# Diagonal tap weights built by ScalarE instead of GpSimd, with three smaller reorderings, in a four-block decoder trunk

## The reference, cut to what matters

```python
for i in range(DEPTH):                       # DEPTH = 2
    x = layer_norm(ALPHA * x + 0.5 * swiglu(x, ffn1_w_gu[i], ffn1_w_down[i]), ...)
    if i % 2 == 0:
        y, qm = gla_mix(x @ gla_w_in, ...)   # gated linear attention
    else:
        y, qm = conv_mix(x @ conv_w_in, ...) # depthwise convolution of width 31, layer norm, silu
    m = mem_attention(qm, mem, mem_w_kv[i])
    x = layer_norm(ALPHA * x + concatenate([y, m]) @ w_out, ...)
    x = layer_norm(ALPHA * x + 0.5 * swiglu(x, ffn2_w_gu[i], ffn2_w_down[i]), ...)

def swiglu(x, w_gu, w_down):                 # w_gu is 1024 x 5632, w_down is 2816 x 1024
    a, b = split(x @ w_gu, 2)
    return (silu(a) * b) @ w_down
```

## Time and profile before

| | us |
|---|---|
| median of 3 runs | 2049.1 |
| lowest and highest | 2047.54 and 2049.7 |
| the profiled execution, its own time | 2050.35 |
| the span in its trace, first to last instruction | 2048.6 |
| TensorE busy in it | 2023.3 (99%) |
| VectorE busy | 1355.9 (66%) |
| ScalarE busy | 811.7 (40%) |
| GpSimd busy | 786.7 (38%) |

### The profile page before, as it was taken

One profiled execution on the slowest core, in us unless ns is written; L12 is line 12 of the kernel. 1 busy time (PEld: TensorE's weight loads), 2 busy tenths in 40 slices (PEclk: granted clock), 3 DMA queues, 4 the chain that ended last, 5 costly groups with the idle time before them and its releaser, 6 DMA issues.

```text
span 2048.6 us, 34293 instructions
## 1 busy us (share of the span) xinstructions
PE 2023.3 (99%) x13509; PEld 1856.2 (91%) x13509; DVE 1355.9 (66%) x1842; ACT 811.7 (40%) x1163; POOL 786.7 (38%) x443
## 2 busy tenths in 40 slices
PE   9999999999999999999999999999999999999998
PEld 9899998988988989999898999989887798999887
DVE  4477774554435768877456877646899886767645
ACT  5433452253423344444234444423353534434422
POOL 1499820033312257881015888001100225877000
PEclk9999999999999999999999999999999999999999
DMA  7545323332211234543232445323544322332232
GB/s 250 185 144 163 123 87 101 101 105 83 63 32 62 93 114 144 164 151 104 99 109 93 161 146 164 105 95 99 185 124 175 103 82 84 102 102 92 89 102 87
DMA packets 229497, 239.13 MB, mean 117 GB/s; under 512 B 5983, under 2 KB 222173, under 8 KB 227612
## 3 DMA queue, kind: packets, MB, share of 16 engines
q1 hardware_dynamic: 228764, 235.68, 35.3%
q10 hardware_dynamic: 640, 2.16, 0.3%
HBM read 215.80 MB, written 22.02 MB: 116 GB/s over the span
## 4 chain that ended last, share of the span: by engine, by line
PE 83%; DVE 5%; POOL 5%; issue 3%; ACT 2%; DMA 1%; DVEq 0%; SPq 0%; ACTq 0%; POOLq 0%
PE bank L1764 11%; PE bank L1766 11%; PE bank L1765 11%; PE bank L1893 10%; PE bank L1894 10%; PE bank L1895 10%; PE bank L1775 4%; PE bank L1776 3%; PE bank L1777 3%; DVE u L1680 2%; POOL xlo L531 1%; ACT whi L662 1%; POOL s L553 1%; POOL diag_tmp L585 1%; PE bank L1799 1%
## 5 line engine op out<-in xcount | busy, mean ns | idle before, releaser
L662 ACT CAST whi<-raw 128x2048 fp32r<-128x2048 f32 (+2 forms) x192 | 325.9, 1699 | 881.6 <-POOL scratch L560 436.4
L1113 DVE TENSOR_TENSOR wlo<-raw,whi 128x2048 fp32r<-128x2048 f32 (+2 forms) x166 | 358.4, 2159 | 243.9 <-ACT whi L662 243.6
L537 POOL TENSOR_TENSOR tiny<-tiny 128x2 f32<-128x2 f32 (+1 forms) x13 | 9.4, 724 | 754.3 <-DVE tiny L1389 754.3
L556 POOL TENSOR_TENSOR raw<-raw 128x512 f32<-128x512 f32 x72 | 220.4, 3062 | 0.0
L1764 PE MATMUL bank<-h_hi,whi 128*128 128x512 f32 x528 | 207.1, 392 | 0.0
L1765 PE MATMUL bank<-h_lo,whi 128*128 128x512 f32 x528 | 205.5, 389 | 0.0
L1766 PE MATMUL bank<-h_hi,wlo 128*128 128x512 f32 x528 | 205.5, 389 | 0.0
L1893 PE MATMUL bank<-t_hi,whi 128*128 128x256 f32 x576 | 163.9, 285 | 2.9 <-DVE bank L1181 2.9
L560 POOL TENSOR_TENSOR scratch<-raw,s 128x512 f32<-128x512 f32 x72 | 149.2, 2072 | 44.2 <-DVE ex_lo L1120 44.2
L1893 PE MATMUL bank<-t_hi,ex_hi 128*128 128x256 f32 x576 | 163.7, 284 | 0.7 <-DVE bank L1173 0.4
L1894 PE MATMUL bank<-xlo,whi 128*128 128x256 f32 x576 | 163.0, 283 | 0.0
(11 more groups left out here) (351 smaller groups left out, 5880.8 us busy)
## 6 DMA issues: line engine op xcount, KB each, us to landing
raw<-in_ffn_w_gu_dram SPq DMA_DIRECT2D x88, 1024.0 KB, 4.9
raw<-in_ffn_w_down_dram SPq DMA_DIRECT2D x32, 896.0 KB, 5.0
raw<-in_ffn_w_down_dram SPq DMA_DIRECT2D x32, 512.0 KB, 3.3
raw<-in_gla_w_in_dram SPq DMA_DIRECT2D x14, 1024.0 KB, 5.1
early_raw<-in_conv_w_in_dram SPq DMA_DIRECT2D x18, 512.0 KB, 4.2
lo_scratch<-early_lo SPq DMA_DIRECT2D x18, 512.0 KB, 3.2
diag_scratch<-diag_tmp SPq DMA_DIRECT2D x8, 1024.0 KB, 8.8
raw<-in_conv_w_in_dram SPq DMA_DIRECT2D x16, 512.0 KB, 5.4
```

The source lines that it names most:

```text
L556: nc.gpsimd.tensor_tensor(a21, a21, a11, ALU.add).then_inc(w_sum, 1)
L662: nc.scalar.copy(whi[:, s, 0:kc, 0:width], raw[:, s, 0:kc, 0:width]).then_inc(hi_ready, 1)
L1113: nc.vector.tensor_tensor(wlo[:, s, 0:kc, 0:width], raw[:, s, 0:kc, 0:width], whi[:, s, 0:kc, 0:width].bitcast(F32), ALU.subtract).then_in ...
```

## The change

There are four parts.

1. **Second tile of mem_w_kv by halves.** It is loaded, rounded, subtracted and used in two halves, as the first one already is.
2. **x_sums.** All four sums of a block wait until x is complete in hi and lo part. Before, in blocks 1 to 3, sum 0 waited for the hi parts of the first half of x alone and sum 1 for all hi parts and half of the lo parts. Sums 2 and 3 now come after `split_lo` of the next tile, not before it.
3. **b_hi_c.** The copy goes from ScalarE to GpSimd, right before GpSimd's subtraction that uses it. ScalarE calls silu once on a single column ahead of the norm, and gives its signal `hi_ready` after the affine steps.
4. **The diagonals.** GpSimd builds none. ScalarE builds set i in `ffn_pair(0, i)` for i = 0 to 7, one tap at a time: block t = 0 ahead of its wait for slot 1 of pair i, block t = 1 after the copies of slot 1 of pair i + 1. ScalarE's loop over the pairs of block 0 is written out. SP's list isn't changed.

```diff
             x_rows = a["x"][0].rearrange("(b p) d -> p b d", p=P)
-            for n in range(1, 8):
+            sp.dma_start(raw[:, 1, 0:4, :], w0[:, 0:4, 256:512]).then_inc(second_loaded, 16)
+            sp.dma_start(raw[:, 1, 4:8, :], w0[:, 4:8, 256:512]).then_inc(raw_loaded[1], 16)
+            for n in range(2, 8):
...
-            for i in range(PLAIN):
-                diagonal(i)
             pool.wait_ge(t_ready, 4)
             for i in range(PLAIN, FK // 2):
                 weight_sums(0, i, 0)
                 weight_sums(0, i, 1)
-                if i < 2 * len(TAPS_K):
-                    diagonal(i)
...
-            pool.wait_ge(hi_ready, CONV_OUT_N + 4)
+            pool.wait_ge(raw_loaded[1], 16 * (CONV_OUT_N // 2 + 4))
+            pool.wait_ge(mo_mm, 2 * HEADS)
+            nc.gpsimd.tensor_copy(b_hi_c[:, :, :], raw[:, 1, :, :]).then_inc(b_hi_done, 1)
+            pool.wait_ge(b_hi_done, 1)
...
+            def diagonal(i, t):
+                g, kc = i // 2, TAPS_K[i // 2]
+                if i == 0 and t == 0:
+                    act.wait_ge(tap_split, 2)
+                elif t == 0:
+                    act.wait_ge(diag_stored, 16 * i)
+                for j in range(kc):
+                    c = t * WIDTH + sum(TAPS_K[:g]) + j
+                    last = nc.scalar.activation(diag_tmp[:, j, t * P:(t + 1) * P], ident[:, :], ACT.Copy,
+                                                scale=(w_tap_lo if i % 2 else w_tap_hi)[:, c:c + 1].bitcast(F32))
+                if t:
+                    last.then_inc(diag_built, 1)
...
                 if sums_next:
                     extra_hi(f, i + 1, 0)
+                if f == 0 and i < 2 * len(TAPS_K):
+                    diagonal(i, 0)
...
                 next_hi(f, i, 1)
                 if sums_next:
                     extra_hi(f, i + 1, 1)
+                if f == 0 and i < 2 * len(TAPS_K):
+                    diagonal(i, 1)
...
-            act.wait_ge(raw_loaded[1], 16 * (CONV_OUT_N // 2 + 4))
-            act.wait_ge(mo_mm, 2 * HEADS)
-            nc.scalar.copy(b_hi_c[:, :, :], raw[:, 1, :, :]).then_inc(hi_ready, 1)
+            nc.scalar.activation(tiny[:, 68:69], ones[:, 0:1], ACT.Silu)
             affine(LN_CONV, 0, range(DK), c_hi, ROW_CG, ROW_CB, ACT.Silu)
+            act.wait_ge(b_hi_done, 1)
+            act.sem_inc(hi_ready, 1)
...
-            def x_sums(f):
+            def x_sums(f, js):
                 base = x_base((None, LN_GLA_OUT, LN_FFN[1], LN_CONV_OUT)[f]) if f else 0
-                for j, (to, plus, minus) in enumerate(T_SUM):
-                    if f:
-                        dve.wait_ge(x_hi_ready, base + (DK if j else DK // 2))
-                        dve.wait_ge(x_ready, base + (0, DK // 2, DK, DK)[j])
-                    else:
-                        dve.wait_ge(x_ready, DK)
+                dve.wait_ge(x_ready, base + DK)
+                for j in js:
+                    to, plus, minus = T_SUM[j]
...
                 if i == 0:
-                    x_sums(f)
+                    x_sums(f, (0, 1))
                 else:
                     x_sums_lo(f)
                 split_lo(FFN_N[f] + 2 * i + 2, 0)
+                if i == 0:
+                    x_sums(f, (2, 3))
```

More of the change, by code:

```diff
@@ L318, in build @@
         fin_mm, fin_act, fin_dve, out_stored = (sem(n) for n in ("fin_mm", "fin_act", "fin_dve", "out_stored"))
-        gain_loaded, fin_rows, rows_centred = (sem(n) for n in ("gain_loaded", "fin_rows", "rows_centred"))
+        gain_loaded, fin_rows, rows_centred, b_hi_done = (
+            sem(n) for n in ("gain_loaded", "fin_rows", "rows_centred", "b_hi_done"))
+        second_loaded, second_hi, second_lo = (sem(n) for n in ("second_loaded", "second_hi", "second_lo"))
         block = ctx.enter_context(nc.Block())
@@ L825, in ffn @@
                     ffn_pair(f, i)
-                with act.Fori(PLAIN, FK // 2 - 1) as i:
-                    ffn_pair(f, i)
+                if f == 0:
+                    for i in range(PLAIN, FK // 2 - 1):
+                        ffn_pair(f, i)
+                else:
+                    with act.Fori(PLAIN, FK // 2 - 1) as i:
+                        ffn_pair(f, i)
                 ffn_pair(f, FK // 2 - 1)
@@ L887, in _ @@
                     nc.scalar.copy(whi[:, 0, 4:8, :], raw[:, 0, 4:8, :]).then_inc(hi_ready, 1)
-            split_hi(0, 1)
+            act.wait_ge(second_loaded, 16)
+            nc.scalar.copy(whi[:, 1, 0:4, :], raw[:, 1, 0:4, :]).then_inc(second_hi, 1)
+            act.wait_ge(raw_loaded[1], 16)
+            nc.scalar.copy(whi[:, 1, 4:8, :], raw[:, 1, 4:8, :]).then_inc(hi_ready, 1)
             for n in range(8):
@@ L1518, in _ @@
             mem_low(range(6, 8))
-            for n in range(1, 10):
+            dve.wait_ge(second_hi, 1)
+            nc.vector.tensor_tensor(wlo[:, 1, 0:4, :], raw[:, 1, 0:4, :], whi[:, 1, 0:4, :].bitcast(F32),
+                                    ALU.subtract).then_inc(second_lo, 1)
+            dve.wait_ge(hi_ready, 2)
+            nc.vector.tensor_tensor(wlo[:, 1, 4:8, :], raw[:, 1, 4:8, :], whi[:, 1, 4:8, :].bitcast(F32),
+                                    ALU.subtract).then_inc(lo_ready, 1)
+            for n in range(2, 10):
                 split_lo(n, n % 2)
@@ L2135, in _ @@
             for n in range(8):
-                if n:
+                if n >= 2:
                     pe.wait_ge(lo_ready, n + 1)
-                if n >= 2:
                     pe.wait_ge(kv_evac, 2 * (n - 1))
@@ L2147, in _ @@
                                 pe.wait_ge(lo_ready, 1)
+                        elif n == 1 and k == 0:
+                            pe.wait_ge(second_lo, 1)
+                        elif n == 1 and k == 4:
+                            pe.wait_ge(lo_ready, 2)
                         for t in range(2):
```

## The result

| | us |
|---|---|
| median of 4 runs | 2098.57 |
| lowest and highest | 2098.27 and 2099.42 |
| the kernel before, beside it (4 runs) | 2049.4 |
| ratio to before, 95% interval | 1.024 [1.0227, 1.0253] |
| span in its trace | 2097.7 |

The change costs 49 us where 64 were forecast.

What follows compares the result with a forecast made beforehand. TensorE, busy 99%, was taken to set the pace, with GpSimd adding 0.9 us a pair in block 0. Terms +67 (diagonals), 0, -5.0 and +1.8 sum to +63.8, giving 2112.9 us against the median; range 2088 to 2134, 70%.

Steps and rivals of the forecast that it cites:

- The rival in which SyncE isn't held: Block 0: sets complete before SP issues the loads ahead of their store, so the wait is free; 2040.5 us, chance 6%.
- The ring: Block 0: loads, GpSimd's sums, ScalarE's split and set, and SP's store run serially; 29.85 us a turn, 29.55 with 7 taps.
- Set 0 ready: Block 0: split of slot 1 ends at 85.1, plus 2.4 of taps, gives 87.5; pair 2's loads go 11 us late.
- store and load: SP's store, then the load behind it until it lands: 10.0 us a turn, bounds 5.8 and 13.
- From the last set to pair 9: Block 0: set 7 at 295.3, then landing, sums and lo part bring pair 9 to 316.6, 65.7 us later than before.
- The slow clock: TensorE's clock falls after idling; covered by the ring for pairs 3 to 8, +1.2 to 1.6 us for the last.
- Second tile: Second tile of mem_w_kv: its 1.1 us wait goes but idle time moves behind it; 0 us, between -0.1 and +0.6.
- x_sums: Before blocks 1, 2 and 3: lo parts shorten by 1.7 us each; -5.0 us, bounds -2.5 and -5.1.
- b_hi_c: Norm of the convolution: hi part earlier, but b_lo_c blocks the second lo part; +1.8 us, bounds -3.3 and +2.5.
- the 0.9 us: Block 0: a pair takes 21.0 us against 20.1 in block 2, put down to GpSimd's weight sums and diagonals.
- the ring's range: Block 0: turns of 24.5 to 33.5 us, giving ends of +24 and +97 us.

Runs made afterwards that it cites:

- both blocks at the first place: Changed kernel, but ScalarE builds both blocks of a set ahead of its wait for slot 1; 2056.75 us, ratio 1.0035.
- -5.5 alone: Kernel before with only the x sums moved behind the last lo part; 2044.86 us, ratio 0.9971.
- +2.5 alone: Kernel before with only b_hi_c copied by GpSimd and silu called ahead; 2052.81 us, ratio 1.0009.

## Why the prediction was right

**The mechanism.** A wait of SyncE for ScalarE's sets, with both loads queued behind it, turned a pipeline into a ring. The waits name it (198.7 us in 8), and moving the store alone takes the 49 us away (2049.39). The rival in which SyncE isn't held needed set i - 1 before the next loads' time, and it comes too late. Not by the 25 us for which SyncE stands, though: slot 0 is free when its low part is done, at 105.59 in VectorE's timeline, and its next load goes out at 115.79, 10.2 us later. Slot 1, free at 114.73, is held 1.5 us.

**The ring, piece by piece.** Set 0 ready: 87.5 forecast, 87.50 measured. Sums of slot 0: 5.15, 5.16. Sums of slot 1: 8.8, 8.76. Split: 3.5, 3.35. Eight taps 2.4, 2.45, and seven 2.1, 2.16. The term that was mis-sized is store and load: 10.0 forecast, 8.16 measured. The DMA issues around 88 us, first the store with slot 0's load, then both loads (a median, so 9.8 for slot 1's):

```profile
diag_scratch<-diag_tmp SPq DMA_DIRECT2D x1, 1024.0 KB, 5.3
raw<-in_ffn_w_gu_dram SPq DMA_DIRECT2D x1, 1024.0 KB, 7.6
...
raw<-in_ffn_w_gu_dram SPq DMA_DIRECT2D x2, 1024.0 KB, 8.7
```

The store (issued first) lands after 5.28 us, slot 0's load 7.61 after its own issue, or 8.0 after the store's, and slot 1's load 9.84 after its own. The sum had taken over the 9.2 of a store *behind* a load and added 0.6 for the second load. But a store in front holds the load up by less (7.6 for the 4.9 alone) than a load in front holds up a store (8.8 for the 3.8 alone), and the second load, behind, hardly delays the first: with both blocks at the first place it goes out 4 to 6 us behind it, and from the third turn on the first still takes 7.4. Seven turns from set 0 to set 7 took 193.1 us, not 207.8 (280.56 less 87.50): 2.1 us less each, of which 1.84 are the landing.

**From the last set to pair 9.** Here two errors met, and the smaller took a little of the larger back. The landing was again 1.84 us short of the sum. But the prediction let TensorE begin a pair 6.2 us after the sums of its slot 0, one product ahead of the last low part, and it begins 7.8 after them (from 128.67, where ScalarE starts its split behind pair 3's sums, to 136.43), because VectorE's list holds back the last product of the pair before. So 14.7 + 1.84 - 1.6 = 14.9 us are the distance from the forecast 316.6 to 301.7, nearly all of it in the landing. It accounts for the whole error of 14.3; the other terms are off by less than a microsecond each. Pair 2 began at 105.65 and not near 108: nothing of pair 1 holds it back, so it starts 4.8 us after its sums, as soon as slot 0's low part is done.

**The slow clock.** The forecast had it hidden in the ring for pairs 3 to 8 and +1.2 to 1.6 at the end. The matmuls stand 50.6 us later at pair 9 and 51.75 at pair 10, so +1.1.

**Second tile.** Forecast 0. Its first matmul comes 1.4 us earlier than the 16.36 of before, at 15.00, where 15.2 was forecast. The third tile's waits (TensorE's timeline) and comes at 22.16, 0.05 from the 22.21 of before:

```profile
22.16 0.39 PE L2178 MATMUL bank<-whi,mem_hi 128*128 128x256 f32 x1 [1.24 <-DVE wlo L1129]
```

The idle time moved behind the second tile, as forecast.

**x_sums.** -5.0 forecast, -5.5 alone; in the changed kernel 1.6, 1.5 and 1.5 us at blocks 1, 2 and 3, with lo parts of 6.23 for 7.91.

**b_hi_c.** +1.8 forecast, +2.5 alone. The step was right in its order (copy to 1617.4, first lo part in between, second blocked) and short by two small sizes: b_lo_c takes 5.09, not 4.57, and the clock of 0.66 behind the longer wait.

**Where it was wrong.** The prediction put the 0.9 us by which pairs of block 0 exceed TensorE's pace down to GpSimd, since it is the busiest engine there. GpSimd's list is only the next limit, worth 0.39; the store's traffic beside slot 1's load comes first, with 0.47. Within the forecast this changed nothing, as those microseconds are covered by the ring. It made the rival in which SyncE isn't held too fast: it gave 2040.5, and the kernel with the store one pair later, in which SyncE hardly waits for a set, took 2049.4. The matmuls in the window 120 to 240 are 726 and not 680, by the same term as the time. And the ends of the ring's range are a little off: by its own bounds eight taps give 24.85 and 33.9 us a turn, where it says 24.5 and 33.5. That changes no chance.

## What to carry to other kernels

When a producer is moved to an engine whose list ties it to the consumer's inputs, follow the store's wait in the DMA queue before counting the work: building that took 5 us a pair cost 49 us, because two loads stood behind its store; with the whole set at the earlier place 42 of them came back. Put a bulk store where its wait is already met and no urgent load is on its way; keeping it off the load gained 5.6 us more here than the order alone. A late input stalls not only its own consumer but whatever stands behind it in the lists of the engines that prepare it. And an engine that is 93% busy is not thereby the limit, nor is it free of blame: look at what it stands for between its instructions. Here limits of 21.0, 20.55 and 20.16 us lay one behind the other, and only the nearest could be felt.

## What the runs showed of the hardware

- Three transfers of 1 MB issued within 1 us by one queue, store, load, load, land after 5.3, 8.0 and 10.7 us from the first issue. A load with a store 0.4 us behind lands after 6.6 to 6.8 us, and the store after 8.7 to 8.9; alone they take 4.9 and 3.8.
- ScalarE's 128 x 128 copy with a column as scale takes 0.31 us in a row of eight (2.45). The Trainium skill, "ScalarE: Activation LUTs", section "What ACT_TABLE_LOAD costs", gives 186 ns + 0.833 ns a column, 93 more for a pointer operand and 93 of overlap: 0.29 us by an estimate from that page. The row agrees within 0.02.
- GpSimd's copy of 128 x 2048 from float32 to the rounded form takes 1.91 us, below the 2.0 to 2.6 that the affine select had suggested. GpSimd's subtraction of the same size takes 4.6 us, or 5.1 when VectorE slips in ahead of it.
- Waits of 3.3, 5.8 and 7.2 us on TensorE were followed by a granted clock of 0.66 to 0.71 over five microseconds, and five waits of 4.5 to 6.0 us by one of 0.50, the lower level throughout. So what such a wait costs behind itself, 2.1 us on average here, doesn't follow its length.
